# Seven of eight block products in sixteen more strips of weights, and all weights through five 1 MB slots

## The chip, the core and the metric

The kernel is one program on one core of one Trainium2 chip. Its time is the device time of one execution in microseconds (us). An execution was also taken by the hardware profiler. The engines are PE (TensorE, matrix multiply), PEld (its weight load), ACT (ScalarE), DVE (VectorE), POOL (GpSimd) and SP (SyncE, which here only issues loads).

## The reference

A trunk of two decoder layers on 256 tokens of width 2048, in float32, with a memory of 256 tokens:

```
mem_n = rmsnorm(mem, mem_norm)
for layer in (0, 1):
    h = rmsnorm(x, g[0])
    mix = even_mixer(h) if layer == 0 else odd_mixer(h)      # 2048 -> 4096 (even), 6144 + 16 (odd), then -> 2048
    x = x + rmsnorm(mix, g[1])
    h = rmsnorm(x, g[2])
    q, k, v = h @ wq, mem_n @ wk, mem_n @ wv                 # all 2048 x 2048
    x = x + rmsnorm(attention(q, k, v) @ wo, g[3])
    h = rmsnorm(x, g[4])
    x = x + rmsnorm((silu(h @ w_gate) * (h @ w_up)) @ w_down, g[5])   # 2048 -> 5632 -> 2048
```

The even mixer is stick-breaking attention (columns q, k, v of its projection) beside a pooling mixer (columns u). The odd mixer is gated linear attention: columns q, k, v, an output gate r, and 16 columns a, from which 1024 forget gates are made.

## The kernel before

**Products.** Each float32 factor is split into a rounded part and a rest (`w_hi`, `w_lo` of the weights, `act_hi`, `act_lo` of the tokens), and a product is three matmuls: hi x hi, hi x lo, lo x hi. One matmul contracts 128 rows for 128 tokens and 512 columns.

**Chunks and strips.** A weight matrix is read in chunks of 512 rows by 512 columns (1 MB; 128 partitions x 2048 values). Sixteen k-tiles of 128 rows are four chunks. A strip is 1024 columns, so 8 chunks: `quad` multiplies four chunks (512 columns) with both halves of the tokens (m = 0, 1), 24 matmuls a chunk, and leaves the sums in PSUM banks 2q and 2q+1. A strip is two quads, q = 0 and 1, with 192 matmuls. Banks 4 to 7 (WORK) serve transposes, scores and other small products.

**Pipeline of a chunk.** SP loads it into `w_raw`, ACT rounds it into one of four slots of `w_hi` (`split` on ACT, L551), DVE subtracts for `w_lo` (`split` on DVE, L973), and PE multiplies (`mm`, L1505, whatever the operands). A slot of `w_hi` is free when PE has used the chunk four before it (`w_used`). In the projections `w_raw` has 4 slots of half a chunk (512 KB): a load waits for `lo_done` of the half chunk that was there. So each chunk is two instructions of 1024 values on ACT and on DVE.

**Seven products.** Only the gate and up projection of the feed-forward (`gu`, 11 strips of 512 + 512 columns a layer) does without one product in eight in its top 1024 rows, from its second strip on. The top two by two blocks of weights B11, B12, B22, B21 are summed on DVE (`add`, L1400; `w_sum`), sums of the tokens' blocks are made once a layer (`token_sums`, L1384 to L1390; `s_hi`, `s_lo`), and chunks 0 to 6 of the strip are one product each (12 matmuls, L1505) into one bank. Between them ACT copies banks (`snap`): PE waits for the first copy before product 2, for the third before product 4, and for the fifth before product 6. Chunks 7 to 10 are plain, 24 matmuls each. There a chunk is loaded whole into one of six `wide` slots, two of which lie in other tensors' room, and split whole: L876 on ACT, L1396 on DVE.

**Order.** Each engine has one queue that runs in order. The program writes the order of each out by hand: in a strip, `pair` on ACT and DVE places a stage's other work (copies of finished banks, the functions `mid` and `end`) between the splits of chunks 4 to 11, the last four of which belong to the next quad. `transposed` stages (k of the memory, q and k of the mixers, the query xq) copy a finished bank into `nat`, PE transposes it into a WORK bank (L1575) in the middle of the next quad (`after_first`), and ACT and DVE copy it out (`take_t`; L605, L1056). `natural` stages (v, u, r) copy banks straight to where they are used. `opening` transposes the normed tokens `y` (L1589) between the matmuls of the first quad. `turn` is the chain between two sublayers: norm, residual, next norm, with POOL's power (`roots`, L416) and one and a half chunks split on POOL (`lo_split`, L437), which is how a stage's first chunks come to PE.

**Order of stages.** mem_norm; mk0, mv0, mk1, mv1; then per layer: mixer (layer 0: sb_qk, sb_z, sb_vu first strip, sb_sum, sb_vu second strip, sb_pv, pool; layer 1: gla_qk, gla_a, gla_at, gla_g, gla_v, gla_s, gla_r first strip, gla_o, gla_r second strip), mix_out, xq, x_s, x_pt, x_pv, x_out, gu, down. In layer 1, gla_a is the product with the 16 columns a, split by hand into `gw_hi` and `gw_lo`; gla_at transposes it; gla_g makes gate inputs of it in the WORK banks; then ACT takes absolute value, exp and log (L770 to L775), DVE a sum of them and eight scans (L1259, L1264, `gla_e` L1271), ACT two exps (`qi`, `ki`, L779, L780). In the middle of gla_v DVE has `state_gates` (L1279), `chunk_forms` (L1283 to L1287), `state_queries` (L1291) and `decayed_queries` (L1296, L1301), and ACT `exp_state` and `exp_query` (L784, L785, L789).

## Time and profile before

| | |
|---|---|
| runs | 3042.12 us median of 3 (3040.94 to 3046.04) |
| profiled execution | 3044.26 us, span 3042.4 us |
| PE busy | 2931.5 us, 96% of the span, 13262 matmuls |
| DVE, ACT, POOL busy | 60%, 47%, 3% |
| mean granted TensorE clock | 0.984 of full |
| moved by DMA | 576.99 MB, mean 190 GB/s |

The span runs from the first to the last instruction; what lies around it, 1.9 us, is part of the execution's time. Mean durations of matmuls overlap (a matmul of 391 ns is followed by the next after less), so their pace is read from runs of many.

### The profile page before, as it was taken

What the parts mean: (1) busy time and instruction counts of PE and PEld (TensorE: products, weight loads), DVE (VectorE), ACT (ScalarE), POOL (GpSimd) and SP (SyncE); (2) the same over time, 40 slices, a digit from 0 to 9 for tenths busy, and PEclk for the clock granted to TensorE, in tenths of its full rate; (3) what the DMA queues carried; (4) which work ended last, traced back from release to release, by engine and by line L of the source; (5) the groups of instructions that cost most, each with busy time, mean ns of one, the idle gap of its engine ahead of it and who ended that gap; (6) DMA issues with size and microseconds to landing.
All of it is one profiled execution on the core that took longest, in us unless ns stands there. A gap on an engine that the chain in (4) does not pass through costs nothing.

```text
span 3042.4 us, 35636 instructions
## 1 busy us (share of the span) xinstructions
PE 2931.5 (96%) x13262; PEld 2428.0 (80%) x13262; DVE 1837.6 (60%) x1537; ACT 1439.4 (47%) x1548; POOL 97.6 (3%) x109
## 2 busy tenths in 40 slices
PE   6999999999999999999998989999999999999998
PEld 5888878887787888887887878777877888887887
DVE  5444444445447888885555535555446988886554
ACT  4433444434335666654444434444334655665443
POOL 0000000001001000000002000001001000000000
PEclk9999999999999999999999979999999999999999
DMA  7665656464345665557554625565435555664653
GB/s 265 213 222 185 221 182 206 153 221 166 139 166 194 221 219 184 185 188 249 193 193 144 194 77 172 194 234 174 159 132 202 196 183 214 221 219 172 210 193 132
DMA packets 254181, 576.99 MB, mean 190 GB/s; under 512 B 14176, under 2 KB 14192, under 8 KB 250080
## 3 DMA queue, kind: packets, MB, share of 16 engines
q1 hardware_dynamic: 249376, 530.63, 50.9%
q0 software_dynamic: 3504, 31.92, 2.6%
q10 hardware_dynamic: 1168, 12.59, 1.1%
q8 instruction: 93, 1.52, 0.2%
q14 instruction: 40, 0.33, 0.0%
HBM read 560.41 MB, written 14.68 MB: 189 GB/s over the span
## 4 chain that ended last, share of the span: by engine, by line
PE 90%; DVE 4%; issue 2%; ACT 2%; POOL 1%; DMA 1%; DVEq 0%; SPq 0%; POOLq 0%; ACTq 0%
PE ps L1505 88%; POOL w_lo L437 1%; DMA w_raw<-in_xattn_wk 1%; DVE w_lo L973 1%; PE ps L1589 1%; PE ps L1575 1%; PE ps L1833 1%; ACT w_hi L551 1%; DVE xres L1088 0%; DMA w_raw<-in_ffn_w_up 0%; DVE wide L1400 0%; DVE y L1084 0%; ACT ps L640 0%; DVE gb L1264 0%; ACT w_hi L876 0%
## 5 line engine op out<-in xcount | busy, mean ns | idle before, releaser
L1505 PE MATMUL ps<-w_hi,act_hi 128*128 128x512 f32 x3632 | 1340.0, 393 | 36.0 <-DVE act_lo L1019 23.0
L1505 PE MATMUL ps<-w_lo,act_hi 128*128 128x512 f32 x3632 | 1333.7, 391 | 0.0
L1505 PE MATMUL ps<-w_hi,act_lo 128*128 128x512 f32 x3632 | 1333.6, 391 | 0.0
L973 DVE TENSOR_TENSOR w_lo<-w_raw,w_hi 128x1024 fp32r<-128x1024 f32 x673 | 797.0, 1222 | 556.7 <-ACT w_hi L551 553.1
L551 ACT ACTIVATE w_hi<-w_raw 128x1024 fp32r<-128x1024 f32 x688 | 694.9, 1052 | 612.0 <-PE ps L1505 453.2
L1505 PEld LDWEIGHTS ps<-w_hi,act_hi 128*128 128x128 f32 x3632 | 685.6, 189 | 183.3 <-issue 30.6
L1505 PEld LDWEIGHTS ps<-w_hi,act_lo 128*128 128x128 f32 x3632 | 685.6, 189 | 143.8
L1505 PEld LDWEIGHTS ps<-w_lo,act_hi 128*128 128x128 f32 x3632 | 686.2, 189 | 141.8 <-issue 0.2
L1396 DVE TENSOR_TENSOR w_lo<-wide,w_hi 128x2048 fp32r<-128x2048 f32 x180 | 410.6, 2289 | 66.1 <-ACT w_hi L876 65.5
L876 ACT ACTIVATE w_hi<-wide 128x2048 fp32r<-128x2048 f32 x180 | 344.3, 1914 | 160.9 <-PE ps L1505 104.6
L1476 DVE TENSOR_TENSOR act_lo<-mid,act_hi 128x256 fp32r<-128x256 f32 x80 | 34.0, 425 | 177.4 <-ACT act_hi L948 177.4
L948 ACT ACTIVATE act_hi<-mid 128x256 fp32r x80 | 33.4, 417 | 223.3 <-PE ps L1505 223.3
L1505 PE MATMUL ps<-w_hi,s_hi 128*128 128x512 f32 x320 | 126.6, 396 | 3.6 <-DVE nat L1377 3.6
L1505 PE MATMUL ps<-w_hi,s_lo 128*128 128x512 f32 x320 | 124.7, 390 | 0.0
L1505 PE MATMUL ps<-w_lo,s_hi 128*128 128x512 f32 x320 | 124.6, 389 | 0.0
L1400 DVE TENSOR_TENSOR w_sum<-wide,wide 128x2048 f32<-128x2048 f32 x40 | 91.7, 2292 | 33.4 <-PE ps L1505 33.4
L876 ACT ACTIVATE w_hi<-w_sum 128x2048 fp32r<-128x2048 f32 x40 | 76.8, 1920 | 69.9 <-DVE w_sum L1400 44.2
L1400 DVE TENSOR_TENSOR wide<-wide,wide 128x2048 f32<-128x2048 f32 x40 | 91.7, 2292 | 2.8
L1396 DVE TENSOR_TENSOR w_lo<-w_sum,w_hi 128x2048 fp32r<-128x2048 f32 x40 | 91.4, 2285 | 0.0
L640 ACT ACTIVATE ps<-ps 128x512 f32<-128x512 f32 x48 | 27.9, 582 | 115.9 <-DVE y L1084 115.9
L1084 DVE TENSOR_TENSOR y<-ps,gain 128x512 f32<-128x512 f32 x48 | 31.9, 687 | 81.4 <-PE ps L1505 58.0
L1505 PEld LDWEIGHTS ps<-w_hi,s_hi 128*128 128x128 f32 x320 | 60.1, 188 | 16.2 <-DVE nat L1377 4.5
(185 smaller groups left out, 1305.7 us busy)
## 6 DMA issues: line engine op xcount, KB each, us to landing
w_raw<-in_ffn_w_down SPq DMA_DIRECT2D x176, 512.0 KB, 4.3
wide<-in_ffn_w_gate SPq DMA_DIRECT2D x80, 1024.0 KB, 10.2
wide<-in_ffn_w_up SPq DMA_DIRECT2D x80, 1024.0 KB, 8.7
w_raw<-in_odd_w_in SPq DMA_DIRECT2D x96, 512.0 KB, 4.4
w_raw<-in_xattn_wk SPq DMA_DIRECT2D x64, 512.0 KB, 4.6
w_raw<-in_xattn_wv SPq DMA_DIRECT2D x64, 512.0 KB, 4.4
w_raw<-in_even_w_in SPq DMA_DIRECT2D x64, 512.0 KB, 4.5
w_raw<-in_xattn_wq SPq DMA_DIRECT2D x64, 512.0 KB, 4.4
```

Of the source, the lines that this page charges most:

```text
L437: nc.gpsimd.tensor_tensor(w_lo[:, at_slot, part], w_raw[:, (2 * s + h) % RAW_SLOTS, :], w_hi[:, at_slot, part].bitcast(F32), ALU.subtract) ...
L551: nc.scalar.activation(w_hi[:, (off + s) % W_SLOTS, h * HALF:(h + 1) * HALF], w_raw[:, slot, :], ACT.Copy).then_inc(hi_done, 1)
L876: nc.scalar.activation(w_hi[:, (c + j) % W_SLOTS, :], src, ACT.Copy).then_inc(hi_done, 2)
L948: nc.scalar.activation(act_hi[:, s % 4:s % 4 + 1, :], mid[:, bass.ds(i * 4 + s, 1), :], ACT.Copy).then_inc(jit_hi, 1)
L973: nc.vector.tensor_tensor(w_lo[:, at_slot, part], w_raw[:, (2 * s + h) % RAW_SLOTS, :], w_hi[:, at_slot, part].bitcast(F32), ALU.subtract)\
L1084: nc.vector.tensor_tensor(y[:, m, cols], ps[:, b, :], gain[:, cols], ALU.mult).then_inc(y_scaled, 1)
L1396: nc.vector.tensor_tensor(w_lo[:, at_slot, :], src, w_hi[:, at_slot, :].bitcast(F32), ALU.subtract).then_inc(lo_done, 2)
L1400: nc.vector.tensor_tensor(out, a, b, ALU.add).then_inc(add_done, 1)
L1476: nc.vector.tensor_tensor(act_lo[:, s % 4:s % 4 + 1, :], mid[:, bass.ds(i * 4 + s, 1), :], act_hi[:, s % 4:s % 4 + 1, :].bitcast(F32), ALU ...
L1505: return nc.tensor.matmul(dst, lhs, rhs, start=start, stop=stop, skip_group_check=loose)
L1575: ins = nc.tensor.transpose(ps[:, b, (k % 2) * T + m * P:(k % 2) * T + (m + 1) * P], nat[:, q, m, k * P:(k + 1) * P], ident[:])
L1589: ins = nc.tensor.transpose(ps[:, WORK + b, k * P:(k + 1) * P], y[:, m, (4 * b + k) * P:(4 * b + k + 1) * P], ident[:])
```

## The change

- `stage` lists for each strip whether it is summed (`Strip.g`). Besides the 20 strips of gu, these 16 are: mk0's second, both of mv0, mk1 and mv1, the second of sb_qk and gla_qk, both of sb_vu and gla_v, gla_r's first, and the second of xq0 and xq1. Each has 11 chunks (`strip11` on PE) with 7 x 12 + 4 x 24 = 180 matmuls. The strips of mix_out and x_out and down stay plain.
- All weights are loaded whole (1 MB) into five `wide` slots in a ring of their own. `slot_free` says for each load which count of `lo_done` or `add_done` (the fourth add of a strip) frees its slot. In gu the fourth sum is made in place, in B21's slot. ACT and DVE split whole chunks (L542, L999), in halves only in a `turn` and at the start.
- `lead` (first four chunks of a strip) and `rest8` or `rest11` (the others) take the place of `pair`, with hooks `before_1`, `before_3`, `before_5`, `before_7`. The left banks of a summed strip go out on ACT (`left_banks`), the right ones on DVE (`right_banks`), which adds a copy that ACT took.
- Token sums (`token_adds`, `token_hi`, `token_lo`) are made in the first strip of mk0, sb_qk, xq0, gla_qk and xq1 too.
- In layer 1 PE does gla_a straight after gla_qk, ahead of the last transposes, and `gw_hi`, `gw_lo` are made in gla_qk's first strip (`gate_rank`).
- The gains, the copy of x and the second operand of the memory (`vx`) are loaded later than before, since their room is used by others. Loops of `transposed`, `natural` and down are unrolled.

```diff
+        pl = plan[name] = dict(at, strips=[])
+        for summed in seven:
+            st = Strip(at["c"], at["n"], at["g"] if summed else None, at["a"], at["u"])
+            pl["strips"].append(st)
+            for k in range(8):
+                if summed and k == B11:
+                    slot_free.append((1, 4 * st.g + 4))
+                else:
+                    chunk = {B12: 4, B22: 5, B21: 6}.get(k, k + 3) if summed else k
+                    slot_free.append((0, 2 * (st.c + chunk + 1)))
+            at["c"] += SUMMED if summed else 8
...
-                    for q in range(2):
-                        for s in range(4):
-                            src = cut(w, s)[:, :, bass.ds(i * (2 * NB) + (col0 + q * NB), NB)]
-                            load(src, i * 8 + c0, 4 * q + s)
+            def load(n, src):
+                if n >= WIDE:
+                    summed, count = slot_free[n - WIDE]
+                    sp.wait_ge(add_done if summed else lo_done, count)
+                dst = wide[n % WIDE][:]
+                if len(src.shape) == 3:
+                    dst = dst.rearrange("p (k n) -> p k n", k=4)
+                sp.dma_start(dst, src).then_inc(wide_full[n % WIDE], 16)
+            def strip(st, w0, col0, w1, col1):
+                order = [(q, s) for q in range(2) for s in range(4)]
+                if st.g is not None:
+                    order = [(0, 0), (1, 0), (1, 1), (0, 1), (0, 2), (0, 3), (1, 2), (1, 3)]
+                for k, (q, s) in enumerate(order):
+                    w, col = ((w0, col0), (w1, col1))[q]
+                    load(st.n + k, cut(w, s)[:, :, col:col + NB])
+            def strips(name, w, col0=0):
+                for i, st in enumerate(plan[name]["strips"]):
...
+            def lead(st, before_1=nothing, before_3=nothing):
...
+                hi(st.c, landed(st.n + B11))
+                before_1()
+                act.wait_ge(add_done, 4 * st.g + 1)
+                hi(st.c + 1, w_sum[:, (st.c + 1) % W_SLOTS, :])
+                act.wait_ge(add_done, 4 * st.g + 3)
+                hi(st.c + 2, wide[(st.n + B11) % WIDE][:])
+                before_3()
+                hi(st.c + 3, landed(st.n + B21))
...
+            def rest11(st, q_sb, p5_sb, reuse=(), before_5=nothing, before_9=nothing):
+                c, g = st.c, st.g
+                act.wait_ge(w_used, c + 1 + W_SLOTS)
+                act.wait_ge(bank_free[1], st.u + 1)
+                nc.scalar.activation(ps[:, 1, :], ps[:, 0, :], ACT.Copy, scale=-1.0).then_inc(snap, 1)
+                act.wait_ge(add_done, 4 * g + 2)
+                hi(c + 4, wide[(st.n + B12) % WIDE][:])
+                before_5()
+                act.wait_ge(w_used, c + 2 + W_SLOTS)
+                for free in reuse:
+                    act.wait_ge(*free)
+                nc.scalar.activation(p5_sb, ps[:, 2, :], ACT.Copy).then_inc(snap, 1)
+                hi(c + 5, landed(st.n + B22))
+                act.wait_ge(w_used, c + 3 + W_SLOTS)
+                act.wait_ge(bank_free[3], st.u + 1)
+                nc.scalar.activation(ps[:, 3, :], ps[:, 1, :], ACT.Copy).then_inc(snap, 1)
+                nc.scalar.activation(q_sb, ps[:, 1, :], ACT.Copy).then_inc(snap, 1)
+                act.wait_ge(add_done, 4 * g + 4)
+                hi(c + 6, wide[(st.n + B21) % WIDE][:])
+                split_wide = lambda j: hi(c + j, landed(st.n + j - 3))
+                split_wide(7)
+                act.wait_ge(w_used, c + 5 + W_SLOTS)
+                act.wait_ge(snap, 5 * g + 4)
+                nc.scalar.activation(ps[:, 1, :], ps[:, 3, :], ACT.Copy, scale=-1.0).then_inc(snap, 1)
+                split_wide(8)
+                before_9()
+                split_wide(9)
+                split_wide(10)
+            def left_banks(st, dsts, func=ACT.Copy, free=()):
+                for m in range(MT):
+                    if m == 0:
+                        act.wait_ge(m0_done, st.a + 1)
+                        for f in free:
+                            act.wait_ge(*f)
+                    else:
...
+            def lead(st, before_1=nothing, before_3=nothing):
...
+                    split(st, 3)
+                    return
+                c, g = st.c, st.g
+                b11, b12, b22, b21 = (src_of(st.n + k) for k in range(4))
+                lo(c, b11)
+                before_1()
+                loaded(st.n + B11)
+                loaded(st.n + B12)
+                dve.wait_ge(w_used, c + 2)
+                add(w_sum[:, (c + 1) % W_SLOTS, :], b11, b12)
+                loaded(st.n + B22)
+                dve.wait_ge(add_done, 4 * g + 1)
+                add(b12, b22, b12)
+                dve.wait_ge(add_done, 4 * g + 2)
+                add(b11, b12, b11)
+                lo(c + 1, w_sum[:, (c + 1) % W_SLOTS, :])
+                lo(c + 2, b11)
+                before_3()
+                lo(c + 3, b21)
...
+            def rest11(st, before_5=nothing, before_7=nothing):
+                c, g = st.c, st.g
+                b11, b12, b22, b21 = (src_of(st.n + k) for k in range(4))
+                dve.wait_ge(add_done, 4 * g + 3)
+                add(b21, b11, b21)
+                lo(c + 4, b12)
+                before_5()
+                lo(c + 5, b22)
+                lo(c + 6, b21)
+                before_7()
+                for j in range(7, SUMMED):
+                    lo(c + j, src_of(st.n + j - 3))
+            def right_banks(st, dsts):
+                dve.wait_ge(snap, 5 * st.g + 5)
+                for m in range(MT):
+                    if m == 0:
+                        dve.wait_ge(m0_done, st.a + 2)
+                    else:
+                        dve.wait_ge(w_used, st.c + SUMMED + W_SLOTS)
+                    nc.vector.tensor_tensor(dsts[m], ps[:, 2 + m, :], dsts[m], ALU.add).then_inc(bank_free[2 + m], 1)
+            def token_adds(name, free=()):
+                s_sum = sums_of(name)[0]
+                for f in free:
...
+                    nx = pl["strips"][i + 1] if i == 0 else nxt
+                    if st.g is None:
+                        own = take_m1(st, 0, nat[:, 0, 1, :], reuse(0))
+                        if i == 0 and name in SUM_STAGES:
+                            rest8(st, before_5, lambda: (token_adds(name, token_free(name)), own()))
+                            token_lo(name)
+                        else:
+                            rest8(st, before_5, own)
+                        lead(nx, take_t(0), take_m1(st, 1, nat[:, 1, 1, :], reuse(1)))
+                    else:
+                        rest11(st, before_5)
+                        lead(nx, nothing, lambda: (right_banks(st, (nat[:, 1, 0, :], nat[:, 1, 1, :])), take_t(0)()))
+                    before_5 = take_t(1)
+                return before_5
...
+                    def gate_rank():
+                        act.wait_ge(gate_in, 16 * 2)
+                        nc.scalar.activation(gw_hi[:], gw_raw[:], ACT.Copy).then_inc(gw_done, 1)
+                    v_strips, r_strips = plan["gla_v"]["strips"], plan["gla_r"]["strips"]
+                    transposed("gla_qk", qk, v_strips[0], gate_rank)()
...
+                    natural(v_strips[0], gv, 0, v_strips[1], exp_state)
+                    natural(v_strips[1], gv, 2 * NB, r_strips[0], exp_query)
...
+                    take_k = transposed("gla_qk", qk, v_strips[0], gate_rank)
                     for m in range(MT):
                         dve.wait_ge(work_full[WORK + m], plan["gla_a"]["rf"] + 1)
                         nc.vector.tensor_copy(a_nat[:, m, :], ps[:, WORK + m, 0:RANK])\
                             .then_inc(bank_free[WORK + m], 1)
+                    take_k()
...
+                    natural(v_strips[0], gv, 0, v_strips[1], state_gates, chunk_forms)
+                    natural(v_strips[1], gv, 2 * NB, r_strips[0], state_queries, decayed_queries)
+                    r0, r1 = r_strips
+                    natural(r0, gr, 0, r1)
...
+            def strip11(st, name, after_0=None, after_3=None, after_9=None):
+                c, snaps = st.c, 5 * st.g
+                _, s_hi, s_lo = sums_of(name)
+                def sums(t):
+                    return s_hi[:, t, :, :], s_lo[:, t, :, :]
+                pe.wait_ge(bank_free[0], st.u + 1)
+                product(c, tokens(0, 0), 0, True).then_inc(w_used, 1)
+                if after_0 is not None:
+                    after_0()
+                pe.wait_ge(bank_free[2], st.u + 1)
+                pe.wait_ge(sums_ready, SUM_STAGES.index(name) + 1)
+                product(c + 1, sums(2), 2, True).then_inc(w_used, 1)
+                pe.wait_ge(snap, snaps + 1)
+                product(c + 2, sums(0), 1).then_inc(w_used, 1)
+                product(c + 3, tokens(4, 0), 0).then_inc(w_used, 1)
+                if after_3 is not None:
+                    after_3()
+                pe.wait_ge(snap, snaps + 3)
+                product(c + 4, sums(3), 3).then_inc(w_used, 1)
+                product(c + 5, sums(1), 2).then_inc(w_used, 1)
+                pe.wait_ge(snap, snaps + 5)
+                product(c + 6, tokens(4, 1), 1).then_inc(w_used, 1)
+                for j in range(7, SUMMED):
+                    q, k = (j - 7) // 2, 8 + 4 * ((j - 7) % 2)
+                    ins = product(c + j, tokens(k, 0), 2 * q)
+                    if j % 2 == 0:
+                        ins.then_inc(m0_done, 1)
+                    product(c + j, tokens(k, 1), 2 * q + 1).then_inc(w_used, 1)
+                    if j == 9 and after_9 is not None:
+                        after_9()
             def transpose_quad(i, pl, q):
...
+                    rest = transposed("gla_qk", "pre_mix1", "gla_qk")
...
                         ins.then_inc(work_full[WORK + m], 1)
+                    rest()
                     for b in (6, 7):
...
-                    natural("gla_v")
+                    for st in plan["gla_v"]["strips"]:
+                        strip11(st, "gla_qk")
```

ACT in layer 1, after the gates' log: first before, then after. `gla_e`, `dec` belong to `exp_state`; L592, L600 are the first two `snap` copies; 128x1024 is half a chunk.

```order
L779 ACTIVATE qi<-gla_e 128x2048
L780 ACTIVATE ki<-gla_e 128x2048
L551 ACTIVATE w_hi<-w_raw 128x1024 x6
L594 ACTIVATE gv<-ps 128x512
L551 ACTIVATE w_hi<-w_raw 128x1024 x4
L784 ACTIVATE gla_e<-gla_e 128x2048
```

```order
L841 ACTIVATE qi<-gla_e 128x2048
L842 ACTIVATE ki<-gla_e 128x2048
L592 ACTIVATE ps<-ps 128x512
L542 ACTIVATE w_hi<-wide_52 128x2048
L846 ACTIVATE gla_e<-gla_e 128x2048
L847 ACTIVATE dec<-gb 128x32
L600 ACTIVATE gv<-ps 128x512
```

A copy that PE waits for now stands behind the two exps, and the next one behind `exp_state`.

DVE in the first strip of xq0, after the change (`s_sum_v` are the token sums, L1150 frees bank 1 for the transposes); before, in the same place, the copy to `nat` stood between `w_lo` of chunks 6 and 7 with nothing ahead of it:

```order
L999 TENSOR_TENSOR w_lo<-wide_52,w_hi 128x2048
L1076 TENSOR_TENSOR s_sum_v<-act_hi,act_lo 128x512 x4
L1080 TENSOR_TENSOR s_sum_v<-s_sum_v 128x512 x3
L1082 TENSOR_TENSOR s_sum_v<-s_sum_v 128x512
L1150 COPY nat<-ps 128x512
L999 TENSOR_TENSOR w_lo<-wide_53,w_hi 128x2048
```

Eight adds now stand ahead of that copy.

DVE at the end of xq0, ahead of the scores: before (with the loop's register instructions), then after.

```order
L1046 COPY nat<-ps 128x512
L1056 ISA
L1056 COPY qx<-ps 128x512
L972 REGISTER_ALU
L973 TENSOR_TENSOR w_lo<-w_raw,w_hi 128x1024
L972 REGISTER_ALU
L973 TENSOR_TENSOR w_lo<-w_raw,w_hi 128x1024
```

```order
L1067 TENSOR_TENSOR nat<-ps,nat 128x512 x2
L1161 COPY qx<-ps 128x512
L999 TENSOR_TENSOR w_lo<-wide_50,w_hi 128x2048
L1161 COPY qx<-ps 128x512
L1463 TENSOR_REDUCE xden<-ps 128x2
```

The last copy of `qx`, ahead of the scores, went from before the split of the next stage's fourth chunk to behind it.

## Rows read from the trace of the kernel before

**Rows 1.** The page: busy time of the engines

```profile
PE 2931.5 (96%) x13262; PEld 2428.0 (80%) x13262; DVE 1837.6 (60%) x1537; ACT 1439.4 (47%) x1548; POOL 97.6 (3%) x109
```

**Rows 2.** Chain of work: start us, us, what; memory strips, a gu strip

```profile
128.73 108.85 PE ps L1505 x480
...
1119.11 40.82 PE ps L1505 x180
```

**Rows 3.** Timeline of DVE, one gu strip: start us, us, what, idle before

```profile
1138.31 2.29 DVE L1400 TENSOR_TENSOR w_sum<-wide,wide 128x2048 f32<-128x2048 f32 x1 [1.15 <-PE ps L1505]
...
1147.44 2.29 DVE L1396 TENSOR_TENSOR w_lo<-wide,w_hi 128x2048 fp32r<-128x2048 f32 x1
1149.64 0.68 DVE L1405 TENSOR_TENSOR q_sb<-ps,q_sb 128x512 f32<-128x512 f32 x1
```

**Rows 4.** Timeline of PE, layer 1: gla_a, a wait in gla_v, gla_s

```profile
1751.99 1.07 PE L1575 MATMUL ps<-ident,nat 128*128 128x128 f32 x8 [0.83 <-issue]
1757.09 0.38 PE L1505 MATMUL ps<-gw_hi,act_hi 128*128 128x16 f32 x1 [4.03 <-DVE gw_lo L1240]
...
1812.06 0.47 PE L1505 MATMUL ps<-w_hi,act_hi 128*128 128x512 f32 x1 [1.91 <-DVE w_lo L973]
...
1882.00 0.69 PE L1505 MATMUL ps<-qi,ki 128*64 128x64 f32 x4 [2.79 <-DVE qd L1301]
```

**Rows 5.** Windows: A:B, us, PE, PEld, DVE, ACT, POOL busy, PEclk, DMA share

```profile
703.00:708.00 5.00, 5.00 (x15) 3.97 (x16) 4.97 (x6) 3.94 (x4) 2.89 (x2) 0.66 0.59 203
...
1757.00:1778.00 21.00, 20.65 (x96) 20.55 (x96) 0.38 (x3) 0.00 (x0) 0.00 (x0) 0.50 0.15 50
```

**Rows 6.** Chain of work, layer 1, around gla_at and gla_g

```profile
1777.77 0.19 DVE a_nat L1244
...
1779.66 7.17 PE ps L1505 x16
```

**Rows 7.** Timelines of ACT (second exp, `exp_state`) and DVE (`chunk_forms`)

```profile
1806.65 1.92 ACT L780 ACTIVATE ki<-gla_e 128x2048 f32<-128x2048 f32 x1
...
1828.05 1.92 ACT L784 ACTIVATE gla_e<-gla_e 128x2048 f32<-128x2048 f32 x1 [3.50 <-DVE gla_e L1279]
1829.87 0.24 ACT L785 ACTIVATE dec<-gb 128x32 f32<-128x32 f32 x1
...
1836.34 2.28 DVE L1283 SCALAR_TENSOR_TENSOR qi<-qi,qk 128x2048 f32<-128x2048 f32 x1
...
1840.74 2.28 DVE L1287 TENSOR_TENSOR qk<-qk,gla_e 128x2048 f32<-128x2048 f32 x1
```

**Rows 8.** Timelines, layer 0: first matmul of sb_vu; ACT's log; DVE

```profile
495.97 0.48 PE L1505 MATMUL ps<-w_hi,act_hi 128*128 128x512 f32 x1
...
502.89 1.49 ACT L747 ACTIVATE sp_t<-sp_t 128x1536 f32<-128x1536 f32 x1
...
506.08 1.29 DVE L1217 TENSOR_TENSOR band<-band,ident 128x512 f32<-128x512 f32 x2
```

**Rows 9.** Timeline of PE at the end of xq0

```profile
799.53 1.07 PE L1575 MATMUL ps<-ident,nat 128*128 128x128 f32 x8 [0.83 <-issue]
801.60 0.67 PE L1505 MATMUL ps<-kx,qx 128*128 128x256 f32 x2 [0.99 <-DVE qx L1056]
```

**Rows 10.** Timeline of DVE: token sums of gu0, first and last

```profile
960.61 2.49 DVE L1384 TENSOR_TENSOR s_sum<-act_hi,act_lo 128x512 f32<-128x512 f32 x4
...
965.31 0.69 DVE L1390 TENSOR_TENSOR s_sum<-s_sum 128x512 f32<-128x512 f32 x1
```

**Rows 11.** Timelines of ACT and PE, first strip of xq0

```profile
725.31 2.01 ACT L551 ACTIVATE w_hi<-w_raw 128x1024 fp32r<-128x1024 f32 x2 [0.62 <-PE ps L1505]
...
736.00 1.03 PE L1575 MATMUL ps<-ident,nat 128*128 128x128 f32 x8
```

**Rows 12.** Timeline of ACT at the start

```profile
21.39 1.06 ACT L551 ACTIVATE w_hi<-w_raw 128x1024 fp32r<-128x1024 f32 x1 [5.87 <-DMA w_raw<-in_xattn_wk]
```

More of the change, by code:

```diff
@@ L1 @@
+from collections import namedtuple
 from contextlib import ExitStack
@@ L378, in _ @@
+                strips(f"xq{l}", wq[l])
+                strips(f"x_out{l}", wo[l])
+                for i, st in enumerate(plan[f"gu{l}"]["strips"]):
+                    strip(st, w_gate[l], i * NB, w_up[l], i * NB)
+                for k in range(FT):
+                    load(plan[f"down{l}"]["n"] + k, w_down[l][k * P:(k + 1) * P, :])
             for m in range(MT):
@@ L1659, in _ @@
                         ins.then_inc(work_full[b], 1)
-                    natural("sb_vu", pairs=[0])
+                    vu_strips = plan["sb_vu"]["strips"]
+                    strip11(vu_strips[0], "sb_qk")
                     pl = plan["sb_sum"]
```

1065 lines of the change are left out of this document (463 added, 602 removed).

## The prediction

> **What bounds it now.** I read the page first: PE is busy 96% of the span [rows 1], and the chain of work runs through its matmuls almost everywhere. So the engines beside it matter only where PE waits for them. In that chain, 480 matmuls of 512 columns in the memory strips take 108.85 us and 180 in a feed-forward strip 40.82 us without a pause [rows 2]: 0.2268 us each. A plain strip of 192 costs 43.5 us, one of seven products 40.8. The trace of before thus already has the new kind of strip; what it does not have is such a strip next to the mixers' other work. PE is idle for 111 us of the span of 3042.4, nearly all of it at the start, at turns and around the mixers.
>
> **What is saved.** 16 strips x 12 matmuls x 0.2268 = 43.5 us, if nothing waits.
>
> **Does such a strip run freely elsewhere?** In gu, DVE starts the first of three adds when PE has finished the strip's ninth chunk, and needs 3 adds and 2 splits, about 2.2 us each when back to back, until `w_lo` of chunk 2 of the next strip ends at 1149.73; its first bank copy then ends at 1150.32 [rows 3]. PE's old strip ended at about 1149.1 (1119.11, plus 36 + 96 matmuls of 0.2268), and product 1, 2.7 us later, needs bank 2. Margin 1.5 us. In a `transposed` stage the transposes stand right behind product 0 and need bank 3 too, which comes 0.6 us later: margin 0.9 us. The natural stages lack gu's two multiplications. A slot's load is asked for at the latest around `w_lo` of chunk 4 or 5 and used four chunks on, more than 10 us later. I count 0 for these, and the rest of the sum is what stands next to the strips.
>
> **gla_a.** Before, the strips ended 0.83 us ahead of 1751.99, and gla_a began at 1757.09 after a wait of 4.03 for `gw_lo` [rows 4]. Both waits and the transposes go from in front of it. All of gla_a ran at a clock of 0.50, 96 matmuls in 20.6 us [rows 5]. Now it starts at full clock. I take some 4.4 us at twice the pace (as long as the clock held before, after the last strip), the rest at the old: 16.2 us. Then transposes at the lower clock 1.9, a DVE copy 0.9, gla_at and its copies 1.6 (1.9 before) and gla_g 7.2 [rows 6]. Its end, called G from here, comes 27.8 us after the strips instead of 1786.8 - 1751.2 = 35.7: **-7.9**. At the old clock throughout it is about -3.4, at full clock to the end about -19.
>
> **gla_v, the largest term.** Before, G was 1779.66 + 7.17 = 1786.8, and ACT's second exp ended at 1808.57, G + 21.8 [rows 6, 7]; nothing in that chain gets shorter. Before, PE had four chunks of 24 matmuls ready, 21.8 us, and waited 1.91 us [rows 4]. Now the first four chunks are products of 12, 10.9 us, and product 2 needs a bank copy that stands on ACT behind the exps. PE does products 0 and 1 (to about G + 6.8, the clock being at half at first) and waits until the copy, 0.6 us, at G + 22.3. From there I follow the queues, 1.92 us a rounding and 2.28 a whole split, sum or product on DVE (durations in [rows 3, 7]). ACT: rounding of chunk 4 to G + 24.2; `w_lo` of it on DVE to 26.5, `state_gates` to 28.8; `exp_state`, 1.92 + 0.24, to 31.1 [rows 7]; second copy, rounding of chunk 5, to 33.7, third copy 34.3. PE has long finished product 3 and starts product 4 there, then 5 and 6. DVE does `w_lo` of 5 and 6 to 39.2, then `chunk_forms`, three of 2.28 us in a row [rows 7], to 46.1, and `w_lo` of chunk 7 to 48.4. So chunk 7 starts at G + 48.4 where an unhindered strip has it at about 20.3. Four plain chunks, 21.8, some 2 us for a lowered clock after these waits, and the second strip with 1.1 us behind `decayed_queries`: gla_s starts at G + 114. Before it started at 1882.00, G + 95.2, its own wait of 2.79 included [rows 4]. That is +18.9, and since the saving above counts 5.4 us for these two strips already, the term is **+24.3 us**.
>
> **sb_vu.** PE starts it at 495.97 [rows 8], finishes products 0 and 1, 24 matmuls, at 501.5 and waits for the copy behind ACT's log, which ends at 504.38: to 505.0. DVE is free after `band` at 507.37, has a sum and a split to do, and product 4 starts at 511.9 and not at 510.4: 3.5 + 1.5 = **+5.0**.
>
> **Ends of sb_qk, xq0, xq1.** At the end of xq0 PE waits 0.83 us, transposes, waits 0.99 [rows 9]; the scores start 2.9 us after the strip. Now DVE's last copy is behind `w_lo` of the next stage's fourth chunk, whose rounding can start only at the strip's end: 1.9 + 2.3 + 0.7 + hops = 5.1; 5.6 after sb_qk, where the next strip is summed. 2 x 2.2 + 2.7 = **+7.1**.
>
> **First strips with token sums.** The eight small adds take 5.4 us [rows 10]. In xq0 rounding of chunk 5 starts at 725.31 and chunk 6's is one chunk (2.7 us in the second pass over the tokens) later: DVE is free at 732.2. With the sums and the copy it gives bank 1 free at 738.2, but PE transposes it at 736.00 [rows 11]. 2.1 us in each of five stages, taken alike: **+10**. Later in those strips PE, thus delayed, meets no second wait.
>
> **Small ones.** At the start chunk 0's second half lands at 21.4 [rows 12], and rounding now starts after the whole, +1. Whole splits have a longer latency than halves where a copy waits behind them (ahead of sb_qk, gla_o, mix_out1): +2.5. gu's token sums start 0.8 us earlier in each layer, since no load is late there: -1.6. Gains loaded late hold DVE up for some 8 us at mix_out and x_out while PE has four chunks, 21.8 us: 0; without that cover it would be 8 each. Half clock after the longer waits: 15 matmuls at 0.66 in a window of 5 us [rows 5] lose 1.7; I add 2 in all.
>
> **Sum.** -43.5 + 24.3 - 7.9 + 5.0 + 7.1 + 10 + 1 + 2.5 - 1.6 + 2 = **-1.1 us** from 3044.26, the profiled execution, which is 2.1 above the median of the runs shown; against that median, 3041. About 0.2%, 6 us, is what a measurement of this kernel can tell from no change.
>
> What a wait of PE costs beyond itself is read from rows: after the waits around 703 to 708 the clock in that window was 0.66, and no more was lost than the 1.7 us above. TensorE: Matmul & The Clock Gate, in the Trainium skill (Part 1, the section on oscillation), says that an idle PE falls back to half its clock and wins it back only by working, so that a wait is paid for again in work at half pace. By that rule taken to its end, the some 45 us of new waits in the sum would cost up to as much again, and the time would be about 3085; the trace bears out the fall, not its size.
>
> **Rivals.**
> (a) Gate block at full clock, first strips without their wait because DVE is ahead: -11 against the sum, and up to -8 more, 3022 to 3030. For it: no idle time is left before gla_a. Against: 0.50 stood through 20 us of dense issue of just these matmuls [rows 5]. Chance 0.25.
> (b) The saving comes whole, since PE passes the gates' chain otherwise hidden: 2999. Against it, ACT's queue order, which nothing can pass. 0.05.
> (c) Slower: DVE is late in the ordinary summed strips. The place is `right_banks`, 1.9 us after a strip's end, against PE's need at 2.7 [rows 3]. If DVE is more than 0.9 us later (a hop more for the fourth sum's order, or a B22 load in a ring of five landing behind the ninth chunk), each of 36 strips pays the excess; at 0.5 us it is +18, 3059, and it decides from 0.2 us on. For it: both margins are thin and a slot fewer than gu's six. Against: gu ran at this margin with two more multiplications. 0.2.
> (d) Slower by the clock: after a wait PE stays at half pace for long, as in gla_a, where 0.50 stood for 20 us of work [rows 5]. After the 15 us wait in gla_v's first strip that would be some 10 us lost, after three more waits a few each: 3060. Against it: after the other waits of before the clock was back within some 5 us. 0.05.
> (e) Forecast, within 6 us: 0.45.
> That the change doesn't do what it says is no case: the order of its matmuls shows 192 fewer.
>
> **Numbers.** Faster: (a) + (b) = 0.3. Slower: (c) + (d) = 0.25. The range, 3025 to 3058, reaches through most of (a) and (c), and leaves out (b), (d) and the far ends; the forecast's own is 3035 to 3048.
>
> **What would show it.** PE's count 192 lower, 13070. Products 2 and 4 of gla_v's first strip waiting for ACT's copies, 15 us and 3; chunk 7 for DVE 6 us. gla_a's windows at 0.50 or 1.00. About 2 us ahead of the first transposes in five stages; scores 5 us after the strip. Strips of the memory at 40.8 plus transposes. It is wrong if gla_v's first strip starts its chunk 7 much before 48 us after gla_g, or if memory strips show waits of their own.

## The result: 0.34% slower, and PE's new waits stand where they were forecast

| | before | changed |
|---|---|---|
| median | 3042.47 us (10 runs, 3040.94 to 3046.26) | 3053.99 us (10 runs, 3049.28 to 3055.68) |
| ratio | 1 | 1.0034, 95% interval 1.0024 to 1.0044 |
| profiled execution | 3044.26 us, span 3042.4 | 3051.12 us, span 3049.4 |
| PE busy, matmuls | 2931.5 us, 13262 | 2901.0 us, 13070 |
| PE idle (span less busy) | 110.9 us | 148.4 us |
| mean granted clock | 0.984 | 0.978 |

The forecast was 3041, no measurable change; the kernel is 11.5 us slower. The time lies inside the range of 3025 to 3058, in the part that belonged to the cases slower than before.

The page of the changed kernel, its span and its engines (to set beside [rows 1]):

```profile
span 3049.4 us, 31694 instructions
...
PE 2901.0 (95%) x13070; PEld 2398.4 (79%) x13070; DVE 2092.8 (69%) x1376; ACT 1541.1 (51%) x1361; POOL 99.6 (3%) x112
```

Three numbers of these rows carry the whole result. PE has 192 matmuls fewer, which at 0.2268 us are 43.5 us. Its idle time grew by 148.4 - 110.9 = 37.5 us. And its busy time fell by only 2931.5 - 2901.0 = 30.5 us, not by 43.5: the matmuls that are left, nearly all of them the same, took 13.0 us longer. -43.5 + 13.0 + 37.5 = +7.0, the difference of the two spans. (The median is 2.9 us above the changed kernel's profiled execution; of its ten runs the profiled one has the highest mean clock, 0.978, the others 0.975 to 0.977. Another profile of the same kernel, below, has 0.975, and 2904.4 us busy, which makes the 13.0 us there 16.4.)

**The waits.** What PE waited for in the changed kernel (who waits and for whom: us in total, times, the longest):

```profile
PE ps L1547 <- ACT ps L592: 18.3, 2, 15.0
...
PE ps L1662 <- DVE nat L1150: 12.5, 5, 2.7
...
PE ps L1547 <- DVE qx L1161: 6.6, 2, 3.3
...
PE ps L1547 <- DVE w_lo L999: 4.1, 2, 3.5
PE ps L1547 <- ACT ps L605: 3.2, 1, 3.2
...
PE ps L1547 <- DVE qk L1161: 3.0, 1, 3.0
```

L592 and L605 are ACT's bank copies in summed strips (gla_v and sb_vu), L1150 the copy of bank 1 behind the token sums (five stages), L1161 the last transposed bank ahead of the scores (xq0, xq1, sb_qk), L999 `w_lo`. Together 47.7 us. None of these rows is from an ordinary summed strip: neither the memory nor gu waits inside its strips.

**gla_v.** PE's timeline of the first strip (start, duration, and in brackets the idle time before it and its releaser), ahead of it the end of gla_g:

```profile
1768.48 7.16 PE L1547 MATMUL ps<-a_t,gate_w_sb 16*128 16x256 f32 x16 [0.55 <-DVE a_t L1360]
1775.58 0.80 PE L1547 MATMUL ps<-w_hi,act_hi 128*128 128x512 f32 x1
...
1797.92 0.79 PE L1547 MATMUL ps<-w_hi,s_hi_x 128*128 128x512 f32 x1 [15.05 <-ACT ps L592]
...
1809.20 0.50 PE L1547 MATMUL ps<-w_hi,s_hi_x 128*128 128x512 f32 x1 [3.24 <-ACT ps L605]
...
1822.70 0.50 PE L1547 MATMUL ps<-w_hi,act_hi 128*128 128x512 f32 x1 [3.46 <-DVE w_lo L999]
```

and ACT's in the same time:

```profile
1793.53 1.91 ACT L841 ACTIVATE qi<-gla_e 128x2048 f32<-128x2048 f32 x1 [9.25 <-DVE gla_e L1384]
1795.47 1.91 ACT L842 ACTIVATE ki<-gla_e 128x2048 f32<-128x2048 f32 x1
1797.29 0.58 ACT L592 ACTIVATE ps<-ps 128x512 f32<-128x512 f32 x1
...
1804.32 1.92 ACT L846 ACTIVATE gla_e<-gla_e 128x2048 f32<-128x2048 f32 x1 [4.63 <-DVE gla_e L1392]
1806.14 0.24 ACT L847 ACTIVATE dec<-gb 128x32 f32<-128x32 f32 x1
1806.28 0.58 ACT L600 ACTIVATE gv<-ps 128x512 f32<-128x512 f32 x1
```

With G = 1775.6 the reader sees the forecast step by step: the copy that PE needs stands behind the two exps and ends at G + 22.3 (forecast 22.3), product 4 starts at G + 33.6 (34.3), chunk 7 at G + 47.1 (48.4). ACT stood idle for 9.25 us just ahead of the exps: it wasn't overloaded, its order was fixed.

**The clock.** Busy times and granted clock of two stretches of the changed kernel: from the end of sb_z (the scores behind sb_qk) through the first three products of sb_vu, and the scores and values of xq0 (columns as in [rows 5], the clock is the third from the right; half clock is one of 0.50). The first pair is from before, the second after:

```profile
480.00:500.00 20.00, 18.17 (x93) 15.22 (x92) 6.57 (x7) 8.49 (x11) 3.12 (x5) 1.00 0.51 160
785.00:835.00 50.00, 45.16 (x208) 38.03 (x207) 20.84 (x38) 16.25 (x33) 0.54 (x1) 0.97 0.30 106
```

```profile
480.00:500.00 20.00, 16.77 (x65) 13.61 (x65) 7.17 (x5) 13.05 (x15) 5.10 (x7) 0.78 0.36 113
785.00:835.00 50.00, 41.46 (x179) 34.31 (x178) 20.17 (x36) 13.00 (x30) 1.07 (x2) 0.90 0.20 71
```

The work in a stretch is not quite the same before and after, since the stages have moved by some us. The same work is the 32 matmuls of sb_z, first before, then after:

```profile
490.74 5.48 PE L1505 MATMUL ps<-qk 128*128 128x256 f32 x32 [0.99 <-DVE qk L1056]
...
476.60 8.04 PE L1547 MATMUL ps<-qk 128*128 128x256 f32 x32 [3.03 <-DVE qk L1161]
```

A wait of 3.03 us stands in front, 2 us more than before, and the work behind it takes 2.6 us longer. That is the shape of the missing 13 us. It doesn't come every time. The other profile of the changed kernel has a clock of 0.93 and 0.90 in the two stretches: there sb_vu's wait of 3.24 us, the same as here, is followed by matmuls at full pace, here by 12 of them at half pace:

```profile
493.34 0.79 PE L1547 MATMUL ps<-w_hi,s_hi_x 128*128 128x512 f32 x1 [3.23 <-ACT ps L592]
493.93 0.63 PE L1547 MATMUL ps<-w_lo,s_hi_x 128*128 128x512 f32 x1
```

### The profile page after: what moved, and what is told of

The parts are those of the page before. It is cut to its first block and busy times, and to the rows that moved or that the text cites. A ratio compares the mean times of both kernels' runs of the same rounds, so it can differ in the third digit from the quotient of the medians.

```text
span 3049.4 us, 31694 instructions
## 1 busy us (share of the span) xinstructions
PE 2901.0 (95%) x13070; PEld 2398.4 (79%) x13070; DVE 2092.8 (69%) x1376; ACT 1541.1 (51%) x1361; POOL 99.6 (3%) x112
## 5 line engine op out<-in xcount | busy, mean ns | idle before, releaser
L999 DVE TENSOR_TENSOR w_lo<-wide,w_hi 128x2048 fp32r<-128x2048 f32 x552 | 1255.9, 2289 | 529.7 <-ACT w_hi L542 527.9
L542 ACT ACTIVATE w_hi<-wide 128x2048 fp32r<-128x2048 f32 x552 | 1053.2, 1914 | 559.8 <-PE ps L1547 456.4
L1547 PE MATMUL ps<-w_hi,act_hi 128*128 128x512 f32 x3312 | 1215.4, 393 | 39.0 <-DVE act_lo L1141 22.5
L1547 PE MATMUL ps<-w_lo,act_hi 128*128 128x512 f32 x3312 | 1209.2, 391 | 0.0
L1547 PE MATMUL ps<-w_hi,act_lo 128*128 128x512 f32 x3312 | 1208.7, 391 | 0.0
L1003 DVE TENSOR_TENSOR wide<-wide,wide 128x2048 f32<-128x2048 f32 x108 | 247.2, 2289 | 5.5 <-DVE w_sum L1003 0.5
L1547 PE MATMUL ps<-w_hi,s_hi_x 128*128 128x512 f32 x544 | 217.5, 400 | 23.8 <-ACT ps L592 18.3
L1547 PE MATMUL ps<-w_hi,s_lo_x 128*128 128x512 f32 x544 | 214.4, 394 | 0.0
L1547 PE MATMUL ps<-w_lo,s_hi_x 128*128 128x512 f32 x544 | 214.2, 394 | 0.0
L1547 PEld LDWEIGHTS ps<-w_lo,s_hi_x 128*128 128x128 f32 x544 | 103.8, 191 | 20.8
L542 ACT ACTIVATE w_hi<-w_sum 128x2048 fp32r<-128x2048 f32 x36 | 69.2, 1922 | 96.8 <-DVE w_sum L1003 96.8
L999 DVE TENSOR_TENSOR w_lo<-w_sum,w_hi 128x2048 fp32r<-128x2048 f32 x36 | 82.2, 2284 | 0.0
```

The costliest lines, as they stand in the source:

```text
L542: nc.scalar.activation(w_hi[:, c % W_SLOTS, :], src, ACT.Copy).then_inc(hi_done, 2)
L999: nc.vector.tensor_tensor(w_lo[:, c % W_SLOTS, :], src, w_hi[:, c % W_SLOTS, :].bitcast(F32), ALU.subtract).then_inc(lo_done, 2)
L1003: nc.vector.tensor_tensor(out, a, b, ALU.add).then_inc(add_done, 1)
L1547: return nc.tensor.matmul(dst, lhs, rhs, start=start, stop=stop, skip_group_check=loose)
```

## The experiments

Theory A: the loss is the listed waits plus the half clock that follows them. Its rivals: that whole splits and a busier DVE make the queues late in general, so that waits would only move; and that five slots or late banks cost the ordinary strips something. Ratios are each to the kernel before on the same chip, with 95% intervals. The changed kernel itself was run again only on the chip of e5 to e7. e1 to e4 ran on another, where the kernel before took 1.8 us more, so "less than the changed kernel" is uncertain by some 2 us there; by the ratios the four are 16, 17, 21 and 21 us less.

**e0_changed.** The changed kernel again, for comparison.

> The changed kernel again, unaltered, so that the others can be set against it on one chip: 1.0034 times the kernel before, within 0.1%.

Measured: 3055.21 us, 1.0033 (1.0024 to 1.0042). Its profiled execution has a span of 3053.5 us:

```profile
PE 2904.4 (95%) x13070; PEld 2401.6 (79%) x13070; DVE 2092.5 (69%) x1376; ACT 1540.5 (50%) x1361; POOL 99.5 (3%) x112
```

**e1_gla_v_plain.** `natural` on ACT, DVE and PE was given plain strips again, with the hooks where they were before:

```diff
-            stage("gla_v", (True, True))
+            stage("gla_v", (False, False))
```

> Both strips of gla_v plain again, 384 matmuls for 360, with the other work where it stood before. Theory A (the loss is PE's new waits plus the half clock that follows them): waits fall by 17.7 us (22.4 in gla_v to 4.7), the half clock after them gives back about 4, 24 matmuls cost 5.4: 16 to 18 us less than the changed kernel, 3036 to 3038. Theory B (ACT's and DVE's queues are late in general with whole splits, and the waits would only move): less than 8 us, 3046 or more.

Measured: 3039.34 us, 0.9982 (0.9973 to 0.9991): 15 to 16 us less than the changed kernel, although PE does 24 matmuls more. The waits of 15.05, 3.24 and 3.46 us are gone, two are left:

```profile
1804.49 0.47 PE L1567 MATMUL ps<-w_hi,act_hi 128*128 128x512 f32 x1 [1.95 <-DVE w_lo L1009]
...
1874.48 0.45 PE L1567 MATMUL ps<-qi,ki 128*64 128x64 f32 x4 [4.42 <-DVE qd L1434]
```

The second is gla_s, as before but 1.6 us longer. Theory A holds for the place: the two summed strips save 5.4 us of matmuls and cost some 21. The time is 1 us above what it expected, since almost nothing came from the clock in this profile: the idle time fell by 16.7 us to 131.7, and the busy time, 2905.9 us, is 4.9 more for the 24 matmuls more (5.4).

**e2_sums_behind.** DVE copies bank 1 before it makes the token sums:

```diff
-                            rest8(st, before_5, lambda: (token_adds(name, token_free(name)), own()))
+                            rest8(st, before_5, lambda: (own(), token_adds(name, token_free(name))))
```

> In the first strips of mk0, sb_qk, xq0, gla_qk and xq1 DVE copies bank 1 ahead of the token sums. Theory A: PE's five waits ahead of the first transposes (2.44 to 2.72 us each, 12.5 in all) fall to 1.6 in all, and the half clock after two of them goes: 12 to 14 us less, about 3041. Theory B: the sums delay the split behind them instead, and half of the waits comes back there: 6 us less, 3048.

Measured: 3037.29 us, 0.9978 (0.9968 to 0.9987), 17 us less than the changed kernel. But the waits did what theory B says: in place of five of 12.5 us in all there are five of 8.0 (1.5 to 1.8 each) one quad later, ahead of the next transposes:

```profile
78.39 1.06 PE L1662 MATMUL ps<-ident,nat 128*128 128x128 f32 x8 [1.77 <-issue]
```

So the time came out better than theory A's number with less of the waits gone. PE was busy for 2891.2 us with the same 13070 matmuls, 10 to 13 us less than in the two profiles of the changed kernel (this profile is of the fastest of the nine executions, 3.6 us below their median). None of the five waits of 1.5 to 1.8 us has half clock behind it in this profile; of the five of 2.4 to 2.7, two have in one profile of the changed kernel and four in the other. The rest of the 10 to 13 us stands behind waits that the edit doesn't touch.

**e3_last_copy_first.** ACT and DVE take the last transposed bank in the hook ahead of the split of the fourth chunk, in sb_qk, xq0 and xq1 (DVE's part):

```diff
-                        lead(nx, nothing, lambda: (right_banks(st, (nat[:, 1, 0, :], nat[:, 1, 1, :])), take_t(0)()))
+                        early = i == 1 and name[:2] in ("sb", "xq")
+                        lead(nx, nothing, lambda: (right_banks(st, (nat[:, 1, 0, :], nat[:, 1, 1, :])), take_t(0)(),
+                                                   take_t(1)() if early else None))
```

> In sb_qk, xq0 and xq1 ACT and DVE take the last transposed bank ahead of the split of the next stage's fourth chunk. Theory A: three waits of 3.0, 3.3 and 3.3 us fall to about 1 us each, as before, -6.5, and with them goes most of 15 us of work at half clock behind them, -5: about 3043. Theory B (only the waits count): -6.5, 3047.5, with the half clock as it was.

Measured: 3034.69 us, 0.9964 (0.9950 to 0.9977), 20 us less than the changed kernel where 11 were expected. The same stretch of sb_z in its timeline:

```profile
474.54 5.47 PE L1554 MATMUL ps<-qk 128*128 128x256 f32 x32 [0.88 <-DVE qk L1164]
```

The wait fell by 2.15 us and the matmuls behind it by 2.57. Busy time is 2894.8 us for 13070 matmuls, 6.2 and 9.6 less than in the two profiles of the changed kernel. The direction and the mechanism are theory A's, the size was again underrated; part of the excess is in stretches that the edit doesn't touch, where the clock of one execution differs from another's. In xq0 the 64 matmuls behind the scores took 15.74 us in both profiles of the changed kernel and 14.05 here, behind the same wait (first the changed kernel):

```profile
816.20 15.74 PE L1547 MATMUL ps<-px,vx 128*128 128x256 f32 x64 [1.58 <-DVE px L1477]
...
807.73 14.05 PE L1554 MATMUL ps<-px,vx 128*128 128x256 f32 x64 [1.58 <-DVE px L1484]
```

**e4_fill.** Every wait stays, but PE works in it, in ten of the twelve (not in gla_v's waits of 3.24 and 3.46 us). One of the places:

```diff
+                if name in ("sb_qk", "gla_qk") and st.u in FILL:
+                    pe.wait_ge(bank_free[3], st.u + 1)
+                    filler(FILL[st.u], 3, c + 2)
                 pe.wait_ge(snap, snaps + 1)
```

> All waits stay in place, but PE does matmuls whose result nobody reads in them: 62 ahead of product 2 of gla_v's first strip, 12 there in sb_vu, 12 or 13 ahead of the scores of sb_qk, xq0, xq1, and 9 ahead of the first transposes of each first strip of a transposed stage. They fit within the waits (0.2268 us each), so nothing gets shorter but the half clock. Theory A: some 25 to 30 us less of PE's work at half clock, 8 to 14 us less time, 3040 to 3046. Rival: the half clock costs no more than the 2 us of the forecast: within 3 us of the changed kernel or slower by the matmuls that don't fit, 3051 to 3058.

Measured: 3036.07 us, 0.9963 (0.9949 to 0.9976), 19 us less than the changed kernel (21 by the ratios), by adding 157 matmuls; theory A had expected 8 to 14. This is the experiment that separates waits from clock: no copy comes earlier, and the waits listed as idle are only relabelled as work. The page, and the two stretches of above:

```profile
PE 2922.1 (96%) x13227; PEld 2415.8 (80%) x13227; DVE 2092.2 (69%) x1376; ACT 1540.8 (51%) x1361; POOL 99.6 (3%) x112
```

```profile
480.00:500.00 20.00, 18.21 (x82) 14.50 (x81) 11.11 (x7) 16.01 (x15) 5.12 (x7) 1.00 0.56 185
785.00:835.00 50.00, 44.95 (x212) 37.89 (x213) 19.11 (x35) 13.90 (x29) 1.07 (x2) 1.00 0.21 79
```

0.78 (0.93 in the other profile) and 0.90 (both) became 1.00. The idle time and the filling together are 3035.7 - 2922.1 + 35.6 = 149.2 us, the idle time of the changed kernel (148.4 and 149.1), so the waits are as long as they were in all. Less the 157 x 0.2268 = 35.6 us of filling, PE's own matmuls took 2886.5 us, 14.5 and 17.9 less than in the two profiles of the changed kernel. The rival (half clock costs no more than 2 us) is out: with waits at these places the clock costs some 16 us of this kernel's time.

**e5_ring_only** and **e6_memory_only.** Fifteen of the sixteen strips plain again (gla_r's first stays), then the memory's seven summed:

```diff
-        stage(f"mk{l}", (l > 0, True), rounds=2)
-        stage(f"mv{l}", (True, True))
+        stage(f"mk{l}", (False, False), rounds=2)
+        stage(f"mv{l}", (False, False))
```

and likewise for sb_qk, sb_vu, xq, gla_qk and gla_v; e6_memory_only keeps the first two lines.

> No summed strip outside gu but gla_r's first (15 of the 16 plain again); what stays is the loading, the splits of whole chunks, the hooks, gla_a ahead of the transposes, the unrolled loops and gla_qk's token sums. Against the kernel before: gla_a -7.4, gla_r -2.7, start -1.4, one wait for token sums +2.4, three last copies behind the fourth split +7 and half clock behind them +4: within 4 us of the kernel before. Rival (five slots of 1 MB hold the plain strips up): waits for loads or w_lo inside plain strips, 10 us or more slower than before.

> As e5_ring_only, but with the seven summed strips of the memory (84 matmuls less). Its price in waits is one, 1.2 us more ahead of mk0's first transposes: 17 to 19 us less than e5_ring_only. Rival (c) of the prediction (each summed strip loses some tenths of a us to late banks): 0.5 us a strip would leave 15.5 or less, with waits inside the strips.

Measured: e5_ring_only 3064.32 us, 1.0062 (1.0048 to 1.0075); e6_memory_only 3050.31, 1.0020 (1.0011 to 1.0029). e5_ring_only missed its expectation by 17 us, and in part for a plain reason: the token sums of mk0, sb_qk, xq0 and xq1 are still made in it, and the expectation counted those of gla_qk alone. The waits are all there:

```profile
PE ps L1689 <- DVE nat L1160: 12.5, 5, 2.7
...
PE ps L1567 <- DVE qx L1171: 6.6, 2, 3.3
...
PE ps L1567 <- DVE qk L1171: 3.3, 1, 3.3
```

No wait for a load is among PE's waits, and ACT waits for loads in two places, 10.1 us in all, where it was 158 us before the change; so its rival (the ring) finds nothing. Against the kernel before, PE is idle for 14.3 us more (125.2 us), and its 12 matmuls fewer (2.7 us) come with 7.3 us more busy time (2938.8), so the clock costs 10.0. The token sums that were left out of the expectation are 8.5 us of the miss, the clock 6 (10 for 4); some 5 stay open. For the memory, PE's row just behind the last strip of mv1, in e5_ring_only and then in e6_memory_only:

```profile
389.72 0.39 PE L1567 MATMUL ps<-ident,vec_rows 16*128 16x16 f32 x2
```

```profile
370.47 0.39 PE L1567 MATMUL ps<-ident,vec_rows 16*128 16x16 f32 x2
```

19.25 us for 84 matmuls, 0.229 each: there the saving came whole. That decides rival (c) of the prediction for the memory's strips, where it would have left 15.5. The medians differ by 14 us where 17 to 19 were expected, with an uncertainty of some 5 (the two intervals), so the total alone would not have told.

**e7_all_three.** e1, e2 and e3 together.

> The edits of e1_gla_v_plain, e2_sums_behind and e3_last_copy_first together; 14 of the 16 strips stay summed. If the three add up (waits and half clock at separate places): 12 to 16, 17 and 15 to 20 us less than the changed kernel, so 3004 to 3012, over 1% faster than the kernel before. Rival (the parts share their gain, the ends of the queues being late anyway): 3020 or more.

Measured: 3015.10 us, 0.9901 (0.9886 to 0.9916), 40 us less than the changed kernel. The three parts alone gave 15, 17 and 20, 52 in all, 12 more than together; the time is 3 us outside the 3004 to 3012 expected. The idle times do add up nearly: they fell by 16.7, 7.6 and 8.8 us alone (33.1) and by 28.4 together. The clock can't: PE's slow matmuls cost the changed kernel 13.0 and 16.4 us in its two profiles, and nothing of that is left in e7_all_three, 2893.2 us for 13094 matmuls where the pace of the kernel before gives 2893.4. Alone the three had taken 2, 12 and 8 us off the mean of the two, more than there was. How much of that excess is scatter of single profiles, and how much was shared, isn't shown.

**e8_fill_more.** e7_all_three with fillers in its remaining waits, and 14 at every opening.

> e7_all_three with unread matmuls in the waits that it still has: 14 at each opening, where PE waits 3.8 us for act_lo (and in the first one 5.3), 12 ahead of product 2 of sb_vu's first strip, 6 ahead of the transposes behind product 0 of the second strips of transposed stages (1.5 to 1.8 us). No wait gets shorter. e7_all_three does some 52 us of its matmuls outside gla_a at half clock; if the waits cause that, about half of it goes: 10 to 13 us less than e7_all_three, 3002 to 3005. Rival (the clock falls in the turns whatever PE does in its waits): 3012 to 3016.

Measured: 3020.24 us, 0.9923 (0.9910 to 0.9937): 5 us slower than e7_all_three (7 by the ratios), where 10 to 13 less were expected. The mean clock rose to 0.988 in the profiled execution, from 0.983, and yet it lost. Not every opening waits: ahead of sb_qk PE had no wait there, and the 14 fillers cost 4.7 us, more than half of that time at half clock:

```profile
377.02 4.72 PE L1574 MATMUL ps<-w_hi 128*128 128x512 f32 x14
```

The 154 fillers are 34.9 us of work. PE's own matmuls took 6.8 us less than in e7_all_three (2921.3 - 34.9 = 2886.4 against 2893.2), but idle time and fillers together are 132.1 us where the idle time was 120.0, so 12.1 us of fillers stood outside waits. A filler pays only inside a wait that is really there, and for what comes after it. The expectation took the fillers at eight openings as hidden, which they weren't.

**e9_gla_a_wide.** e7_all_three with a wide matmul ahead of every second k-tile of gla_a.

```diff
                         for kt in range(KT):
+                            if kt % 2:
+                                filler(1, WORK + 2, plan["gla_v"]["c"])
```

> e7_all_three with 16 unread matmuls of 512 columns spread among gla_a's 96 of 16 columns. If what lowers the clock there is that the matmuls are so narrow, it stays at 1.00, and gla_a (about 18 us at 0.50) takes 14.3 with the 16 more, and transposes and gla_g after it 4 less: 6 us less in all, 3009. If the clock falls all the same, the 16 cost 3.6 to 7 us, 3019 to 3022.

Measured: 3018.32 us, 0.9917 (0.9904 to 0.9931), 3 us slower than e7_all_three, which is not beyond the intervals, and 9 above the 3009 expected if the clock held. gla_a and what follows it:

```profile
1731.40:1738.00 6.60, 6.60 (x49) 6.25 (x48) 3.58 (x3) 1.91 (x1) 0.00 (x0) 0.92 0.52 171
1738.00:1745.00 7.00, 7.00 (x30) 6.61 (x31) 0.17 (x1) 0.00 (x0) 0.00 (x0) 0.50 0.36 133
```

The clock falls to 0.50 all the same, with PE busy without a pause. What it is about gla_a that lowers the clock stays open; one wide matmul among six narrow ones doesn't prevent it.

**e10_copy_earlier.** e7_all_three with the wait that e2 left: the copy of bank 3 in front of `w_lo` of chunk 2 of the second strip.

```diff
+                before_2()
                 lo(c + 2, b11)
                 before_3()
...
-                        lead(nx, take_t(0), take_m1(st, 1, nat[:, 1, 1, :], reuse(1)))
+                        lead(nx, take_t(0), before_2=take_m1(st, 1, nat[:, 1, 1, :], reuse(1)))
```

> e7_all_three with the copy of the right bank (L1163) moved ahead of w_lo of chunk 2 on DVE in the second strips of mk0, sb_qk, xq0, gla_qk, xq1, where PE still waits 1.5 to 1.8 us ahead of the transposes behind product 0. If that copy is what they wait for: five waits of 8 us in all fall below 2, and some half clock with them, 6 to 9 us less than e7_all_three, 3006 to 3009. If the wait moves on to product 2, whose w_lo is now 0.7 us later: 2 us less or nothing.

Measured: 3006.25 us, 0.9876 (0.9858 to 0.9894), 8 us (by the ratios) or 9 less than e7_all_three. All five waits of 1.5 to 1.8 us are gone, and none has come at product 2. The gain is idle time alone, 109.1 us where it was 120.0; the busy time, 2894.8 us, is 1.6 more, so the half clock that was expected to go with these waits didn't. (One of the four executions took 7538.94 us, the other three 3005.07 to 3006.90, and their median is 3005.60; nothing recorded explains it, and no other kernel had one.)

**e11_first_plain.** e10_copy_earlier with the first strips of sb_vu and gla_v plain and their second ones summed.

```diff
-            stage("sb_vu", (True, True))
+            stage("sb_vu", (False, True))
...
-            stage("gla_v", (True, True))
+            stage("gla_v", (False, True))
```

> e10_copy_earlier with sb_vu's first strip plain too, and gla_v's second strip summed again (first plain). sb_vu: 12 matmuls more (+2.7), two waits of 3.2 and 1.2 us and the half clock behind them go: about 3 us less from sb_vu to sb_pv. gla_v: 12 matmuls less (-2.7), but DVE has chunk_forms (6.9 us) and the three adds in one quad: if it keeps ahead, 2.7 us less from gla_g to gla_s; if not, PE waits for w_lo by up to 4 us, 1 us more. In all 2 to 6 us less than e10_copy_earlier, 3000 to 3004.

Measured: 3000.99 us, 0.9864 (0.9847 to 0.9880), the lowest median, though its interval overlaps that of e10_copy_earlier: 1.4% less than the kernel before and 1.7% less than the changed one. From sb_vu's first matmul to sb_pv's PE now needs 2.4 us less, as expected. gla_v's second strip gives little: to gla_s it is 0.5 us more, and up to gla_r's first matmul 1.5 us less, where 12 matmuls are 2.7. PE waits for DVE's splits there, the case that the expectation named as its rival: 7.7 us in four waits in the whole kernel, against 2.5 in e10_copy_earlier:

```profile
PE ps L1576 <- DVE w_lo L1012: 7.7, 4, 2.9
```

## Why the prediction was wrong, step by step

| step | forecast | profile of the changed kernel |
|---|---|---|
| 16 strips, 192 matmuls | -43.5 | 192 fewer; -19.25 for the 84 of the memory (e6 against e5) |
| gla_v, to the start of gla_s | +24.3 | 112.7 us from G where it was 95.2, +5.4: +22.9 |
| gla_a to G | -7.9 | 28.3 us where it was 35.7: -7.4 |
| sb_vu | +5.0 | +5.4 to +6.4 in the two profiles |
| ends of sb_qk, xq0, xq1 | +7.1 | waits 3.0 + 3.3 + 3.3, less 3 x 0.99: +6.6 |
| token sums | +10 | 12.5 us of waits, less mk0's 1.56 of before: +10.9 |
| half clock elsewhere | +2 | +8.2 in one profile, +15.0 in the other (e0_changed) |

The last row is read from the clock records of the traces. In the changed kernel PE was busy for 102.5 us at half clock (113.6 in e0_changed), in the kernel before for 78.3. Without gla_a to gla_g, gla_v and sb_vu, whose share of it is in the rows above, that is 59.6 and 73.1 against 43.2, and work at half clock costs half of its time.

The places, the releasers and the lengths of the waits were right, down to 1.3 us in a chain of 48. gla_a kept its clock for some 4.3 us and then had 0.50, as taken:

```profile
1747.34 0.17 PE L1547 MATMUL ps<-gw_hi,act_hi 128*128 128x16 f32 x1
...
1747.00:1752.00 5.00, 5.00 (x44) 4.92 (x43) 4.34 (x5) 1.91 (x1) 0.00 (x0) 0.96 0.00 0
1752.00:1766.00 14.00, 13.74 (x64) 13.34 (x64) 0.57 (x3) 0.60 (x1) 0.00 (x0) 0.50 0.00 1
```

The step that failed is the last of the small ones: "15 matmuls at 0.66 in a window of 5 us [rows 5] lose 1.7; I add 2 in all." One stretch of before was taken as the price of all the new waits together. It was the price of one. The changed kernel has twelve new or longer waits of 2.4 us and more (five first transposes, three score blocks, sb_vu, and three in gla_v). In each of its two profiles nine of the twelve have half clock behind them, not the same nine, with 3.0 to 6.2 us of PE's work in it, which costs 1.5 to 3.1 us each; one of them:

```profile
410.20:413.60 3.40, 3.40 (x12) 2.92 (x11) 3.40 (x2) 2.96 (x3) 0.00 (x0) 0.50 0.24 42
```

With 8.2 in place of 2 the sum is +5, against +7 of that profiled execution; with 15.0 it is +12, against +11 of the other and +11.5 of the medians.

Of the rivals, (d), slower by the clock, had the right cause and the right side, with a chance of 0.05; it looked for the loss mainly behind the one long wait of gla_v, some 10 us, where it was 2.5 (4.9 us of work at half clock), while it stood behind the many short ones. What was cited from TensorE: Matmul & The Clock Gate of the Trainium skill (Part 1, the section on oscillation), that each wait is paid for again, was set aside as too large at 45 us more. The runs put it between: e4_fill gave back 19 us without shortening a wait. (c), the thin margins of ordinary summed strips, is refuted by the memory's 19.25 us, and for gu by its strips, which start 41.7 us apart in the changed kernel, as they did before (from 1119.11 in [rows 2] to 1160.81; first before, then the changed kernel):

```profile
1160.81 40.85 PE ps L1505 x180
...
2389.84 40.84 PE ps L1547 x180
...
2431.55 40.82 PE ps L1547 x180
```

(a) and (b) did not occur. Two of the losses, token sums and last copies, were a matter of order on DVE and ACT alone, and gla_v's and sb_vu's of one or two strips left plain: in e10_copy_earlier and e11_first_plain 14 of the 16 strips are summed, and the saving comes through.

## What to carry to other kernels

Split PE's time into three: matmuls times pace, idle, and what busy time exceeds the first. The third is the clock's, and it belongs in the sum once for every new wait of 2.4 us or more, not once in all: here 1.5 to 3 us behind three waits in four of 2.4 to 15 us. A change that halves PE's work in a stage halves the cover of what the other engines do beside it: list every copy that PE now needs there, and what is ahead of it in its queue. A copy that PE waits for goes ahead of any split or sum that PE needs only chunks later.

## What was not expected of the hardware

Adding 157 matmuls whose result nobody reads made a kernel 19 us faster (0.9963 against 1.0033 of the kernel before), with every copy where it was. The profiled executions of one kernel differ in mean clock (0.975 and 0.978) and with it in span (3053.5 and 3049.4), a scatter of 0.13% that no wait explains (their idle times differ by 0.7 us); it lies in which of the same waits has half clock behind it. And gla_a's clock fell to 0.50 with PE busy all through, also with wide matmuls mixed in; why is open.
